# A wider, split output-gate product, an earlier gather and a re-cut last piece in a hybrid encoder layer

## What is computed

```python
proj = h @ w_in                      # columns q_a k_a v_a q_h i_h zf_fwd zf_bwd z_g
o = gated_linear_scan(forward) + gated_linear_scan(backward)
o = o * rsqrt(mean(o^2) + eps) * norm_g * silu(z_g)          # z_g: the output gate
h = layer_norm(ALPHA * h + concat([attn, o]) @ w_out, ln1_g, ln1_b)
for e in range(32):                                           # weights 12.6 MB an expert
    hid = h @ w_up[e] + b_up[e]
    act = min(hid[::2], 7) * sigmoid(1.702 * min(hid[::2], 7)) * (clip(hid[1::2], -7, 7) + 1)
    out = out + gate[:, e] * (act @ w_down[e] + b_down[e])
out = layer_norm(ALPHA * h + out, ln2_g, ln2_b)
```

## Time and profile before

| | us |
|---|---|
| median of three runs | 1087.07 |
| the profiled execution | 1087.5 |
| its span, first to last instruction | 1085.8 |
| first product of `hidden(0)` (L1606) | 166.93 |
| first load that waits for `chunk_used` | 171.06 |
| last instruction of VectorE starts | 1081.87 |

### The profile page before, as it was taken

How to read it: one execution, slowest core, us unless ns; L and a number is a source line. 1 busy time by engine, 2 the same in 40 slices (tenths; PEclk the granted TensorE clock), 3 DMA queues, 4 the chain that set the end, 5 groups by cost and what they waited for, 6 DMA issues and landing times.

```text
span 1085.8 us, 12732 instructions
## 1 busy us (share of the span) xinstructions
PE 1037.2 (96%) x5174; PEld 454.8 (42%) x5174; DVE 256.9 (24%) x670; ACT 194.5 (18%) x366; POOL 8.0 (1%) x25
## 2 busy tenths in 40 slices
PE   8999999999999999999999999999999998899995
PEld 8988664333333333333333333333333333333331
DVE  6886463111111111111111111101111111111113
ACT  5674221111111111111110111101111111011110
POOL 2000000000000000000000000000000000000000
PEclk9999999999999999999999999999999999999999
DMA  9826897999999999999999999999999999999993
GB/s 326 233 68 181 350 409 311 411 426 428 430 433 432 427 435 430 430 432 429 429 435 428 429 434 431 432 432 428 434 433 427 432 432 428 434 430 425 427 422 158
DMA packets 36464, 428.34 MB, mean 395 GB/s; under 512 B 3952, under 2 KB 17312, under 8 KB 20320
## 3 DMA queue, kind: packets, MB, share of 16 engines
q1 hardware_dynamic: 34848, 427.17, 94.1%
q10 hardware_dynamic: 1568, 0.44, 0.2%
HBM read 426.03 MB, written 1.05 MB: 393 GB/s over the span
## 4 chain that ended last, share of the span: by engine, by line
PE 64%; DMA 34%; DVE 1%; ACT 0%; issue 0%; DVEq 0%; SPq 0%; ACTq 0%
DMA ring<-in_w_down_dram 23%; PE bank L1606 23%; PE bank L1672 15%; DMA wbuf<-in_w_down_dram 7%; PE bank L1556 4%; PE bank L1288 4%; DMA tail_mem<-in_w_down_dram 4%; PE bank L1541 3%; PE bank L1305 3%; PE bank L1351 3%; PE bank L1549 1%; PE bank L1650 1%; PE bank L1617 1%; PE bank L1636 1%; PE bank L1333 1%; PE bank L1269 0%
## 5 line engine op out<-in xcount | busy, mean ns | idle before, releaser
L1606 PE MATMUL bank<-ring,wbuf 128*64 128x512 f32 x1248 | 278.1, 595 | 1.3 <-DMA ring<-in_w_up_dram 1.3
L1672 PE MATMUL bank<-ring,wbuf 128*64 128x512 f32 x640 | 151.9, 628 | 19.8 <-DMA ring<-in_w_down_dram 19.0
L1606 PEld LDWEIGHTS bank<-ring,wbuf 128*64 128x64 f32 x1248 | 87.5, 137 | 162.9 <-issue 151.9
L715 ACT ACTIVATE wbuf<-wbuf 128x256 f32<-128x256 f32 x64 | 26.7, 416 | 450.8 <-DVE wbuf L1213 450.8
L1672 PEld LDWEIGHTS bank<-ring,wbuf 128*64 128x64 f32 x640 | 51.7, 144 | 117.0 <-issue 113.2
L1197 DVE TENSOR_SCALAR hT<-iota_s,hT 128x128 f32<-128x128 f32 x64 | 19.3, 343 | 340.1 <-PE bank L1636 339.8
L1213 DVE TENSOR_SCALAR wbuf<-bank 128x256 f32<-128x256 f32 x64 | 26.9, 420 | 304.9 <-PE bank L1606 304.9
L1606 PE MATMUL bank<-tail_mem,wbuf 128*64 128x512 f32 x416 | 93.0, 594 | 0.0
L1606 PE MATMUL bank<-wbuf 128*64 128x512 f32 x384 | 85.8, 594 | 0.0
L1556 PE MATMUL bank<-wbuf,putT 64*128 64x512 f32 x264 | 65.6, 616 | 0.7 <-ACT wbuf L720 0.7
L1541 PE MATMUL bank<-X,hT 128*64 128x512 f32 x256 | 60.9, 593 | 0.0
(11 more groups left out here) (264 smaller groups left out, 811.4 us busy)
## 6 DMA issues: line engine op xcount, KB each, us to landing
ring<-in_w_up_dram SPq DMA_DIRECT2D x29, 4096.0 KB, 40.0
ring<-in_w_down_dram SPq DMA_DIRECT2D x14, 4096.0 KB, 37.6
ring<-in_w_up_dram SPq DMA_DIRECT2D x20, 2048.0 KB, 14.6
wbuf<-in_w_up_dram SPq DMA_DIRECT2D x10, 4096.0 KB, 40.0
tail_mem<-in_w_up_dram SPq DMA_DIRECT2D x9, 4096.0 KB, 40.5
wbuf<-in_w_down_dram SPq DMA_DIRECT2D x5, 4096.0 KB, 36.4
ring<-in_w_down_dram SPq DMA_DIRECT2D x8, 2048.0 KB, 14.0
tail_mem<-in_w_up_dram SPq DMA_DIRECT2D x8, 2048.0 KB, 19.0
```

Of the source, the lines that this page charges most:

```text
L715: a.activation(sig[:, w], glu[:, w], ACT.Sigmoid, scale=SIG_ALPHA).then_inc(s["sig_ready"], 1)
L1606: ins = mm(bank[n][c * SLOTS:(c + 1) * SLOTS, :], xT[:, k, :], units(row, n, c), start=(k == 0), stop=(k == KT - 1))
L1672: ins = mm(bank[1 if last else 2][c * SLOTS:(c + 1) * SLOTS, :], actT[:, at:at + SLOTS], wk[:, a * D + c * 512:a * D + (c + 1) * 512], sta ...
```

## The change

**Output gate.** The two `zg` units are multiplied together, 512 columns wide, in three products of rounded parts: `("zg", 0)`, `("zg", 1)` and `("zg", 2)` in `STEPS` take the place of the two `proj zg` steps, with `zg 1` put between `kpT 1` and `aT 0`. ScalarE makes the high parts of the weights (`zg_rounded`) and of hT (`z_high`), VectorE the low parts. The recurrent half of `w_out` is then loaded only when all of `zg` is done, after chunk 2; chunk 3 follows it, and the bias DMA comes after both.

**Transition.** The first gather takes the centred, unscaled X; the scale `rstd` goes into `pick`, the LayerNorm's bias is added by VectorE where ScalarE copied before, and the four `normed` come after the routing. Fewer `keep_warm`.

**Passes.** The bias product of `hidden` stands after k = 2 instead of k = 0. The first `scatter` is halved, with its second half after the first chunk of `hidden(1)`; the turning of act and gates there comes one k later.

**Tail.** The last four of the last down products go by column halves, c = 0 first, into two banks; copy and scatter follow by halves; ScalarE computes sums for rows 128-255, VectorE for the others.

```diff
-        STEPS += [("proj", "zg", 0)] + two("kpT", 1) + two("aT", 0) + two("aT", 1) + [("lnT", 0, 0)] + two("pT", 3)
-        STEPS += [("proj", "zg", 1), ("pv", 1, 0), ("kv", 0, 0), ("kv", 1, 0)]
+        STEPS += [("zg", 0, 0)] + two("kpT", 1) + [("zg", 1, 0)] + two("aT", 0) + two("aT", 1) + [("lnT", 0, 0)] + two("pT", 3)
+        STEPS += [("zg", 2, 0), ("pv", 1, 0), ("kv", 0, 0), ("kv", 1, 0)]
...
+            def zg_rounded(h, u, freed):
+
+                act.wait_ge(win_in[u % WBUF], 16 * (u // WBUF + 1))
+                act.wait_ge(s["proj_done"], freed + 1)
+                a.copy(zg_high[:, h], w_raw(u).rearrange("p (k n) -> p k n", k=KT)).then_inc(s["zg_high_ready"], 1)
...
+                for t in range(TT):
+                    for k in range(KT):
+                        ins = mm(proj_bank("zg", t)[:, :].rearrange("p (h n) -> p h n", h=2), hp[:, k, t * P:(t + 1) * P],
+                                 wp[:, :, k, :], start=(i == 0 and k == 0), stop=(i == 2 and k == KT - 1))
...
-                v.tensor_scalar(pick[:, t, :], iota_s[:, 0, :], key[:, t, 0:1], None, ALU.is_equal).then_inc(s["picked"], 1)
+                v.tensor_scalar(pick[:, t, :], iota_s[:, 0, :], key[:, t, 0:1], rstd[:, t:t + 1],
+                                ALU.is_equal, ALU.mult).then_inc(s["picked"], 1)
...
+            dve.wait_ge(s["gath_done"], 1)
+            v.tensor_tensor(xg, bank[0][:, :], xg, ALU.add).then_inc(s["xg_ready"], 1)
...
-                keep_warm(bank[0], (0, 9)[t])
+                keep_warm(bank[0], (0, 3)[t])
...
-            hidden(1, {1: lambda: act_turned(0), 2: lambda: gates_turned(0, first=True)})
+            hidden(1, {1: lambda: scatter(start=True, some=(2, 3)), 2: lambda: act_turned(0),
+                       3: lambda: gates_turned(0, first=True)})
...
+                    if last and i == DNC - 1:
+                        pairs = pairs[0:4] + [(a, c) for c in range(2) for a in (2, 3)]
...
-            scatter(last=True)
+            scatter(last=True, some=(0, 2))
+            pe.wait_ge(s["y_ready"], npass + 2)
+            scatter(last=True, some=(1, 3))
```

More of the change, by code:

```diff
@@ L69, in encoder_layer @@
     GI = {g[0]: n for n, g in enumerate(GROUPS)}
-    UNITS = [(n, h) for n, _, w in GROUPS for h in range(w // 256)]
+    UNITS = [(n, h) for n, _, w in GROUPS for h in (range(w // 256) if n != "zg" else (1, 0))]
     UI = {u: i for i, u in enumerate(UNITS)}
@@ L276, in encoder_layer @@
         STEPS += two("x1T", 0) + two("x1T", 1) + two("logit", 0) + two("logit", 1)
-        jobs = [x for x in STEPS if x[0] not in ("first", "proj", "mix", "logit")]
+        jobs = [x for x in STEPS if x[0] not in ("first", "proj", "zg", "mix", "logit")]
         J = {j: n for n, j in enumerate(jobs)}
@@ L761, in _, with totalled @@
             gates_turned(last_pass, b=0)
-            summed(last_pass * CHUNKS + used(down_at(-1, DNC - 1)) + DNC, b=1)
-            for t in range(TT):
-                ln_std(2, t)
+            act.wait_ge(s["y_half"], 1)
+            a.copy(ysb[0:SLOTS, :], bank[1][0:SLOTS, :]).then_inc(s["y_ready"], 1)
+            act.wait_ge(s["chunk_used"], last_pass * CHUNKS + used(down_at(-1, DNC - 1)) + DNC)
+            a.copy(ysb[SLOTS:P, :], bank[3][SLOTS:P, :]).then_inc(s["y_ready"], 1)
+            def totalled(f, m, **how):
+                for n in range(2):
+                    act.wait_ge(s["scat_done"], 2 * n + 2)
+                    tick(a.activation((xg, glu)[n], bank[6 + n][:, :], f, accum_out=tot[:, m, n:n + 1], **how))
+                settle()
+                link(a.activation(tot2[:, m:m + 1], tot[:, m, 0:1], ACT.Identity, bias=tot[:, m, 1:2]))
+            totalled(ACT.Identity, 0)
+            a.activation(negm[:, :], tot2[:, 0:1], ACT.Identity, scale=-1.0 / D).then_inc(s["mean_ready"], 1)
+            ln_std(2, 0)
+            act.wait_ge(s["mean_ready"], 1)
+            totalled(ACT.Square, 1, bias=negm[:, 0:1])
+            a.activation(rstd[:, 1:2], tot2[:, 1:2], ACT.Sqrt, bias=epsc[:, 0:1], scale=1.0 / D).then_inc(s["std_ready"], 1)
         @block.vector
@@ L1128, in _ @@
             inverted(1)
-            normed(1, 0)
             logits(1)
@@ L1132, in _ @@
             keys(1)
-            normed(1, 1)
             v.tensor_copy(bsel[:, :], trio[:, 0:1].broadcast_to([P, SLOTS])).then_inc(s["picked"], 1)
@@ L1155, in _ @@
             v.tensor_reduce(cnt[:, 4:5], cnt[:, 1:4], AX_X, ALU.add).then_inc(s["ex_ready"], 1)
-            dve.wait_ge(s["gath_done"], 1)
+            dve.wait_ge(s["lnb_in"], 16)
+            dve.wait_ge(s["cent_ready"], 2 * TT)
+            for t in range(TT):
+                for n in range(2):
+                    normed(t, n)
             for t in range(TT):
@@ L1550, in gather_turned, with scatter @@
                 ins.then_inc(s["xT_ps"], 1)
-            def scatter(start=False, last=False):
-                for q in range(4):
+            def scatter(start=False, last=False, some=(0, 1, 2, 3)):
+                for q in some:
                     r = slice((q % 2) * SLOTS, (q % 2 + 1) * SLOTS)
@@ L1627, in put_back @@
                 pe.wait_ge(s["put_ready"], p + 1)
-                scatter(start=isinstance(p, int) and p == 0)
+                scatter(start=isinstance(p, int) and p == 0, some=range(2 if isinstance(p, int) and p == 0 else 4))
                 if isinstance(p, int) and p == RESIDUAL:
```

123 lines of the change are left out of this document (83 added, 40 removed).

## The result

The kernel before ran at 1087.26 us (median of four, 1087.04 to 1088.03) beside the changed one at 1102.94 us (median of four, 1102.63 to 1104.78). The ratio is 1.0141, with a 95% interval of 1.0129 to 1.0154: slower by 15.7 us, where 1101.5 was forecast. The profiled execution of the changed kernel took 1102.63 us with a span of 1100.9.

What follows compares the result with a forecast made beforehand. The DMA stream bounds the kernel, its start set by TensorE's head. From 1087.5: +13.7 (bias DMA) + 1.4 (clock) - 1.0 (transition) - 0.4 (sixth release) + 0.7 (tail) = 1101.9, as median 1101.5; range 1092 to 1106.

Steps and rivals of the forecast that it cites:

- The gate's products: Head, TensorE: 48 products of 512 columns at 0.22 us make 10.6 us, saving 3.5 us on TensorE alone.
- the rival at 0.44: Head: wide fp32r products run at the float32 pace, 0.44 us each, giving 1106.5 us; chance 0.06.
- VectorE, ScalarE, `aT`: Head: four subtractions (6.9 us) move `bias_rest` to 101.3, casts to 103.6, second `aT` half to 108.0; `zg` ends 2.3 later.
- The bias DMA: Head: queued behind chunk 2, w_out and chunk 3, the copy lands at 130.5, 13.7 us later; bounds 10.7 and 15.0.
- The lower bound of this term: Bias DMA: landing at 127.5, four transfers at 430 GB/s from 110.2 plus 1.5 us of completion; shift 10.7 us.
- The rival "the copy overtakes": Head: bias copy lands 3 to 4 us after its issue (115), giving 1089.6 us; chance 0.08.
- The rival "faster": Head: copy lands by 113.3 and the wide products win 3.5 us, giving 1081.5 us; chance 0.04.
- The clock: Head: restarts after TensorE's pauses of 5 and 11 us can be at 1.2 GHz; 1.4 us lost, bounds 0 and 3.
- Transition and passes: From head to last pass: transition 1.0 us earlier (bounds 0 and 1.6), sixth release 0.4 earlier.
- The sixth release: Second pass: keeps both scatter halves and the bias, loses only the turning of gates; binds the stream, 0.4 us won.
- Tail: Behind the last down products: products by column halves make it 0.7 us later, range -1.9 to +1.2.
- the order on one half: Tail: neighbouring products on the same half cost 0.44 each; second down half 1.3 later, bank 7 complete some 1.6 later.

Runs made afterwards that it cites:

- e12: Changed kernel with 20 dummy products ahead of the second `aT` half and 42 ahead of the third `kv` step; 1100.89 us, ratio 1.0112 to before.
- e2: Changed kernel with `bias_rest` and `shared(3)` moved ahead of the gate's four subtractions on VectorE; 1098.03 us, ratio 1.0082 to before.
- e6: Changed kernel with 28 dummy products ahead of the second `aT` half and 58 ahead of the third `kv` step; 1105.89 us, ratio 1.0148 to before.
- e1: Changed kernel with the bias DMA issued ahead of the second half of w_out and chunk 3; 1091.38 us, ratio 1.0026 to before.
- e7: Changed kernel with the moves of e1 and e2, and the first scatter whole ahead of `hidden(1)`; 1086.63 us, ratio 0.9984 to before.
- e10: Changed kernel with the edits of e1, e2, e7 and e8 together; 1083.80 us, ratio 0.9960 to before.
- e11: As e10, but with the tail as before the change; 1085.43 us, ratio 0.9973 to before.
- e9: Changed kernel with the moves of e1 and e2, and `down` and scatter products in runs of two on one array half; 1088.14 us, one run.
- e8: Changed kernel with the moves of e1 and e2, and six dummy products instead of three ahead of the second rank product; 1085.00 us, ratio 0.9963.

## Why the prediction was right

**The gate's products.** 0.22 each was estimated, 3.5 us a third; each third has its next work 3.75 to 3.85 us after its start at the full clock, 0.235 to 0.24 a product, near the upper bound; the rival at 0.44 is out (its time adds up to 1106.3, not 1106.5). It made no difference to the forecast of the changed kernel: the pause ahead of `aT` absorbed the first two thirds, and the last only made w_out's issue later.

**VectorE, ScalarE, `aT`.** `bias_rest` was forecast for 101.3 and came at 101.13, the casts for 103.6 (103.44), the second `aT` half for 108.0 (107.92). Here the chain worked because each link was in a row: who was queued behind whom, and for what bank TensorE waits.

**The bias DMA.** Forecast: issued near 114.5, landed at 130.5. It was issued at 117.26 and landed so that VectorE began at 130.99. The issue was 2.8 late, for the most part because of the clock behind the first pause: from the second `aT` half to the gate's last third it took 3.7 us where 2.0 was forecast and e12 has 2.1, and the third itself 4.5 instead of 3.5 (3.9 at the full clock). The landing was only 0.5 late, because it hangs on the bytes from chunk 2's issue on: 16.5 + 4.9 us were forecast, 21.1 measured. The four kernels with w_out and chunk 3 ahead of the copy bear that out: the copy lands 20.4 to 21.5 us behind chunk 2's issue (the changed one, e2, e6, e12), whether w_out is issued 4.8 us behind chunk 2 or 6.3 us; each time that is before chunk 2 has landed. The lower bound of this term also took 1.5 us for a completion, which no row shows by itself; the shortest time from issue to landing of the 512 KB was 3.4 us (e1). TensorE's second pause was 8.65 us where 11 were forecast, since TensorE came to it 2.7 late itself. e1 shows this term alone (11.3 us with the pause's clock), e2 what the later `bias_rest` costs (5.0).

The rival "the copy overtakes" is out: it took 13.7 to 15.6 us behind three loads, 8.9 before, 3.4 to 4.6 behind one, and it landed 1.2 to 2.0 us after the load directly ahead of it (1.2 us before and in the changed kernel: chunk 2 at 115.6 and the copy at 116.8, chunk 3 at 129.7 and the copy at 131.0). That is the second half of the rule of the Trainium skill that the prediction weighed (DMA: Bandwidth & Descriptors, Queues, rings and completion order); the trace agrees with it, and shows nothing of the first half. The rival "faster" is out as well, since the copy would have had to land by 113.3.

**The clock.** 1.4 was taken; e12 gives 2.05, of which 0.34 comes through the landing and 1.7 behind it, within the bounds of 0 to 3. The copy reached VectorE 14.1 us later than before instead of 13.7, and 14.1 + 1.7 is the head's +15.8.

**Transition and passes.** This step failed. Up to the start of `hidden(0)` -1.0 was the term and -0.8 came; the rest of the -1.2 at the first released load is the bias product, which now stands behind it. The sixth release was to come 0.4 earlier against the start of `hidden(0)`, and came 0.5 later (30.86 us behind it instead of 30.34): it keeps both halves of the scatter, which I had counted as 0.9 each and which take 1.1 each, and I hadn't asked what the whole scatter hid, VectorE's 0.61 us. With the whole one in its place (e7) it is 29.8 us. From the sixth release to the last half chunk the changed kernel took another 0.4 us more, and with the whole scatter e10 and e11 show no shorter way there than the kernels with halves, so the rest of the loss in the passes is open. In sum transition and passes won nothing, against 1.4 forecast. The first released load came at 185.68 where 184.6 was forecast; that is the 0.7 us of the head and the 0.2 of the transition, and 0.2 because the bias product's place is worth 0.43 there and not 0.6.

**Tail.** +0.7 was the term, -0.8 came. The mis-sized part is the order on one half (+1.3 to +1.6): it costs nothing (e9). It wins nothing either: the copy of the first half of y starts 2.34 us after the last half chunk, the whole copy started 2.36 after the earlier trace rows. The gain is ScalarE's. It takes the second token tile's statistics while VectorE normalises the first, as the changed kernel's tail shows beside the earlier trace rows:

```profile
1088.76 0.58 ACT L784 COPY wbuf<-bank 64x512 f32<-64x512 f32 x1 [4.92 <-PE bank L1749]
...
1095.15 0.30 ACT L800 ACTIVATE rstd<-tot,epsc 128x1 f32<-128x1 f32 x1
```

```profile
1093.95 1.41 DVE L1303 SCALAR_TENSOR_TENSOR X<-X,rstd,wbuf 128x512 f32<-128x512 f32 x2
1095.48 1.41 DVE L1295 SCALAR_TENSOR_TENSOR X<-bank,negm,wbuf 128x512 f32<-128x512 f32 x2
1096.99 1.41 DVE L1303 SCALAR_TENSOR_TENSOR X<-X,rstd,wbuf 128x512 f32<-128x512 f32 x2
```

ScalarE is done at 1095.45, 0.1 us after VectorE has finished the first tile (1095.36). The rule on parallel tiles (the Trainium skill, TensorEngine Tiling (Array Packing), Key Properties) was read too far: that different tiles run in parallel does not say that two products on the same tile in a row are slower here, and e9 measured that they are not.

In sum: +15.8 - 1.2 + 1.3 - 0.8 = +15.1 between the profiled executions (1087.5 and 1102.63), where 14.4 were forecast. Single terms were off by 0.2 to 1.5 us. That the two largest misses, +1.5 in transition and passes and -1.5 in the tail, cancel is luck; the mechanism that makes up all of the loss was the one forecast, and its two terms (bias DMA and clock, 15.1) were 0.7 short.

## What to carry to other kernels

When TensorE's work in a dense head is made shorter by giving VectorE and ScalarE more, look first at what stands behind the new instructions in their lists, and at the DMA whose issue ends that chain. On one queue a small copy that many wait for must be issued ahead of the large loads that nobody waits for yet: here its place was worth 11 us, nine times what its 512 KB need at 430 GB/s (1.2 us). And a step that looks as if it only filled time (a scatter, a few dummy products) may cover a wait or hold up the clock; before it is cut, look at what ends just behind it.

## What the runs showed of the hardware that I had not expected

- After TensorE's waits of 4.6 and 8.7 us the granted clock was 0.50 in the windows from 110 to 112 and from 134 to 136. It was 1.00 in both places when dummy products filled them (e6, e12). It also fell to 0.50 to 0.60 at the first gather in six kernels, though TensorE had stood for no more than 0.41 us at a time there; with three dummy products more it stayed at 1.00 (e8, e10, e11), though chance is not excluded.
- A fp32r product with 512 columns takes 0.235 to 0.24 us at the full clock, where a float32 product of the same shape is two instructions of 0.44 each (the next work stands 3.54 us behind the start of eight). Three split products (0.71 us) are cheaper than the float32 one (0.88 us).
- A DMA of 512 KB on SyncE's queue landed 1.2 to 2.0 us after the load issued directly ahead of it (changed kernel 1.2, e1 2.0), never before it.
- Products on 64 columns of the array in the order a a b b took 7.11 us for 32, in the order a b a b 7.09.
